# A projection block's stores issued by ScalarE behind its evictions, in a hybrid attention and mLSTM layer

## The reference, cut to what matters

```python
xn = rms_norm(h, norm_mix_w[l])
proj = jnp.einsum('bsd,de->bse', xn, w_in[l])
(da_q, da_k, da_v, ml_q, ml_k, ml_v, ml_i, ml_f, ml_o, gate_pre) = jnp.split(proj, split_idx, axis=-1)
oa = diff_attention(qa, ka, va, lam, cos, sin)     # 8 heads, causal, two softmaxes a head
hm = mlstm_chunkwise(qm, km, vm, i_pre, f_pre)     # 8 heads, after a short causal convolution
merged = g[:, :, 0] * ya + g[:, :, 1] * yb         # ya, yb: both outputs projected
h = h + jnp.einsum('bsd,de->bse', merged, w_out[l])
u = jax.nn.relu(jnp.einsum('bsd,df->bsf', hn, w_ff1[l]))
h = h + jnp.einsum('bsf,fd->bsd', u * u, w_ff2[l])
```

## Time and profile before

| | |
|---|---|
| median of 3 runs | 1978.75 us |
| profiled execution | 1974.37 us, of which the span is 1972.6 us |
| granted TensorE clock, mean | 0.997 |
| TensorE (PE) matmuls | 1910.6 us, 97% |
| VectorE (DVE) | 1190.3 us, 60% |
| ScalarE (ACT) | 965.5 us, 49% |
| GpSimd (POOL) | 383.9 us, 19% |
| stores `proj_d<-ev` | 128 of 256 KB |

### The profile page before, as it was taken

One profiled execution on the slowest core, in us unless ns is written; L12 is line 12 of the kernel. 1 busy time (PEld: TensorE's weight loads), 2 busy tenths in 40 slices (PEclk: granted clock), 3 DMA queues, 4 the chain that ended last, 5 costly groups with the idle time before them and its releaser, 6 DMA issues. The chain is left out here.

```text
span 1972.6 us, 26074 instructions
## 1 busy us (share of the span) xinstructions
PE 1910.6 (97%) x9378; PEld 1598.0 (81%) x9378; DVE 1190.3 (60%) x1538; ACT 965.5 (49%) x1634; POOL 383.9 (19%) x211
## 2 busy tenths in 40 slices
PE   5999999999999999989999999999999999999998
PEld 4788888788888787878888888888888888888886
DVE  6755666566575757553412112278777677789874
ACT  4355565556465556544434322226666765533341
POOL 4221212112121121211213444440000000021002
PEclk9999999999999999999999999999999999999999
DMA  5562747554444546274446453655686686563422
GB/s 152 87 179 57 162 68 152 78 131 107 119 108 115 117 68 166 57 160 99 65 97 213 134 154 92 222 187 211 208 297 225 223 298 211 209 231 132 159 82 86
DMA packets 207826, 291.79 MB, mean 148 GB/s; under 512 B 36841, under 2 KB 127593, under 8 KB 200833
## 3 DMA queue, kind: packets, MB, share of 16 engines
q1 hardware_dynamic: 195856, 282.21, 51.6%
q10 hardware_dynamic: 11888, 8.49, 1.3%
HBM read 203.56 MB, written 87.10 MB: 147 GB/s over the span
## 5 line engine op out<-in xcount | busy, mean ns | idle before, releaser
L730 PE MATMUL gp<-r1h,w_hi 128*128 128x512 f32 x1152 | 454.6, 395 | 6.0 <-ACT ev L1076 3.7
L732 PE MATMUL gp<-r1h,w_lo 128*128 128x512 f32 x1152 | 450.0, 391 | 0.0
L731 PE MATMUL gp<-r1l,w_hi 128*128 128x512 f32 x1152 | 449.4, 390 | 0.0
L1973 POOL TENSOR_TENSOR w_lo<-w_raw,w_hi 128x1024 fp32r<-128x1024 f32 x87 | 218.3, 2510 | 852.2 <-ACT w_hi L1071 852.2
L730 PEld LDWEIGHTS gp<-r1h,w_hi 128*128 128x128 f32 x1152 | 216.8, 188 | 49.7 <-issue 4.1
L732 PEld LDWEIGHTS gp<-r1h,w_lo 128*128 128x128 f32 x1152 | 216.5, 188 | 46.2
L731 PEld LDWEIGHTS gp<-r1l,w_hi 128*128 128x128 f32 x1152 | 216.9, 188 | 41.8
L991 PE MATMUL scores<-xh,qh 128*128 128x512 f32 x512 | 200.1, 391 | 0.6 <-ACT res L1372 0.6
L995 PE MATMUL scores<-xh,ql 128*128 128x512 f32 x512 | 199.2, 389 | 0.0
L993 PE MATMUL scores<-xl,qh 128*128 128x512 f32 x512 | 199.2, 389 | 0.0
L1214 ACT ACTIVATE pr<-scores,nb 128x256 f32<-128x256 f32 (+7 forms) x128 | 93.8, 738 | 118.3 <-DVE nb L1607 116.7
(11 more groups left out here) (342 smaller groups left out, 3745.5 us busy)
## 6 DMA issues: line engine op xcount, KB each, us to landing
xraw<-xo_d SPq DMA_DIRECT2D x54, 1024.0 KB, 5.2
proj_d<-ev SPq DMA_DIRECT2D x128, 256.0 KB, 4.3
rq<-in_w_ff SPq DMA_DIRECT2D x32, 1024.0 KB, 7.8
w_raw<-in_w_in SPq DMA_DIRECT2D x56, 512.0 KB, 9.0
xo_d<-res SPq DMA_DIRECT2D x78, 256.0 KB, 3.3
xo_d<-ring SPq DMA_DIRECT2D x60, 256.0 KB, 2.9
pr<-proj_d SPq DMA_DIRECT2D x16, 512.0 KB, 5.4
gt<-proj_d SPq DMA_DIRECT2D x32, 256.0 KB, 2.8
```

What stands on the lines that cost most here:

```text
L730: pe.matmul(gp[half][:], wh[slot][:, k, :], mh[:, k, t], start=(k == 0), stop=False)
L731: pe.matmul(gp[half][:], wh[slot][:, k, :], ml[:, k, t], start=False, stop=False)
L732: mm = pe.matmul(gp[half][:], wl[slot][:, k, :], mh[:, k, t], start=False, stop=(k == KT - 1))
L1973: pool.tensor_tensor(wl[slot][:], raw[slot][:], wh[slot][:].bitcast(F32), ALU.subtract).then_inc(w_split, 1)
```

## The change

`evac` no longer counts `ev_ready` up: it issues the store itself, on ScalarE's queue. `store` and its calls on SP are gone. In the gate part, where a pair of `oa` loads stood behind each half's store, SP waits on `gp_free` for the same eviction instead. The wait on `st` ahead of the eviction stays, and so do the waits on `st` ahead of SP's loads of `proj_d`.

```diff
-        ev_ready = [sem(f"ev_ready{i}") for i in range(2)]
...
-            def store(n, behind=None):
-
-                for i in range(2):
-                    sp.wait_ge(ev_ready[i], n + 1)
-                    sp.dma_start(proj_d[bass.ds(n, 1), :, i * HALF:(i + 1) * HALF].rearrange("a p n -> (a p) n"),
-                                 ev[i][:]).then_inc(st[i], 16)
-                    if behind:
-                        behind(i)
...
             def head_round(h, att, first=False, second=False, last=False):
                 for b in range(HB):
-                    if b >= 2 or not first:
-                        store(h * HB + b - 2)
...
             for j in range(16):
-                store(N_GATE + j - 2, oa_loads if j == 14 else None)
+                if j == 14:
+                    for i in range(2):
+                        sp.wait_ge(gp_free, 2 * (N_GATE + j - 2) + i + 1)
+                        oa_loads(i)
...
-            for k in range(2):
-                store(N_PA - 2 + k)
...
                 act.activation(ev[half][:], gp[half][:], ACT.Copy).then_inc(gp_free, 1)
                 act.wait_ge(gp_free, 2 * n + half + 1)
-                act.sem_inc(ev_ready[half], 1)
+                act.dma_start(proj_d[bass.ds(n, 1), :, half * HALF:(half + 1) * HALF].rearrange("a p n -> (a p) n"),
+                              ev[half][:]).then_inc(st[half], 16)
```

## The result

| | before | after |
|---|---|---|
| median, 12 runs each, same chip | 1978.10 us (1974.50 to 1983.69) | 1985.43 us (1981.85 to 1989.06) |
| profiled execution, and its span | 1974.37 us, 1972.6 us | 1984.96 us, 1983.1 us |

The ratio is 1.0036, 95% interval [1.0027, 1.0045]: 7.1 us slower by the ratio, 7.3 us by the medians, where 3.7 us were forecast. The time is inside the likeliest case's own range.

What follows compares the result with a forecast made beforehand. TensorE bounds the kernel, its matmuls covering 780.55 of 808 us, so only its waits through ScalarE count. Added 13.0 less removed 9.3 is 3.7 us, on the 1978.75 us median 1982.5 us; range 1970 to 1993.

Steps and rivals of the forecast that it cites:

- the likeliest case: Added 13.0 us and removed 9.3 us nearly balance: 1982.5 us, own range 1976 to 1988, chance 0.42.
- The price of an issue: On ScalarE's list, one store issue costs between 0.34 and 0.51 us, taken as 0.43 us.
- k2: Issue behind eviction k2 delays the exponential and TensorE's L885, already late: all of 0.43 us a round arrives.
- k3: Issue behind eviction k3 delays `w_hi`, so `w_lo`, `nb` and L885, which has no slack: 0.43 us a round.
- k4 and k5: Issues make ScalarE 0.69 us late, passed through `otmp` and tile 5's exponential to `atl`; less 0.12 slack, 0.57 us a round.
- k7: Issue behind eviction k7 delays `ath` and the splitting behind it; TensorE already stalls on that `atl`: 0.43 us a round.
- Together 3.96 + 3.64 + 1.7 = 9.3 us: Gain: waits ahead of k2 in three rounds, the gate part's stall at 877.79 us, and its lower clock vanish.
- The third rival: Stores land as late on ScalarE's queue: none of the 9.3 us goes, 13.0 come, 1991.8 us; chance 0.08.
- What is late next there: nothing on SP: Where store waits vanish, no SP item behind the removed store is late next, so the 9.3 us count as gained.
- The wait that SP gets in the gate part is ... nothing: SP's new gate-part wait is for the eviction whose store it waited for before, so it costs nothing.
- SP's long issues hold ScalarE's: Slower rival: ScalarE's issue near k2 waits for SP's long row-load issue, 8.4 us more, 1990.9 us; chance 0.25.
- The transfers gain more: Faster rival: round 3's `qraw` load lands in time, another 4.6 us gained; 1970 to 1975, say 1971 us; chance 0.25.

Runs made afterwards that it cites:

- run 1: The kernel before, but ScalarE issues the stores of k2, k3, k5 and k7 in the seven rounds, SP all others: 1985.13 us, ratio 1.0037.
- run 3: The kernel before, stores on SP, plus a 4 KB DMA to a scratch tensor issued by ScalarE behind each eviction of the rounds: 1995.19 us, ratio 1.0085.
- run 7: The changed kernel, with the waits and store issues of k2, k3, k4, k5 and k7 moved behind work TensorE waits for: 1968.65 us, ratio 0.9955 to before.
- run 9: The kernel before, with ScalarE's wait for its own eviction and signal to SP moved later for k2, k3, k4, k5 and k7: 1972.64 us, ratio 0.9961.
- run 5: The kernel before, but ScalarE issues the stores of k0, k1, k10 and k11 of each round and the first gate block: 1974.98 us, ratio 0.9985.
- run 4: The kernel before, but ScalarE issues the stores of k0 and k1 of each round and the first gate block: 1979.81 us, ratio 1.0011.
- run 8: The changed kernel, but SP issues the 32 stores of the gate part, ScalarE those of the eight heads: 1984.35 us, ratio 1.0036 to before.

## Why the prediction was right, and where it was not

- **The price of an issue** (0.43 us in place): right. 0.25 to 0.68 and 0.33 to 0.76 us. Runs 1, 3, 7 and 9 show that it is the place that costs: with five of each round's twelve issues set later, a round is as short as without any issue in these places (103.75 and 103.66 us).
- **k2** (0.43): 0.36 in the changed kernel, 0.38 alone. Right.
- **k3** (0.43): 0.30. Mechanism as said, somewhat smaller.
- **k4 and k5** (0.57, on `atl`): ScalarE was 0.69 us late there, as worked out, but the way was another. The step "it passes this on, through the exponential of tile 5 to `atl`" overlooked the `w_hi` behind k5. `w_lo` and the `kqs` operation behind it on GpSimd are late with it, VectorE's `nb` lasts until that ends, and TensorE stalls ahead of it, on `scores` for `pr`. The slack of 0.12 us at `atl` doesn't count on that way: 0.70 us. GpSimd and VectorE after, in round 5; `nb` ends at 599.46 us, and the first exponential starts at 599.50:

```profile
594.69 2.40 POOL L1963 TENSOR_TENSOR w_lo<-w_raw,w_hi 128x1024 fp32r<-128x1024 f32 x1 [20.09 <-ACT w_hi L1060]
597.05 2.39 POOL L1998 TENSOR_TENSOR kqs<-kqs,sg 128x1024 f32<-128x1024 f32 x1
```

```profile
597.75 1.71 DVE L1597 TENSOR_SCALAR nb<-mx 128x2 f32<-128x2 f32 x1
```

- **k7** (0.43): 0.41. Right.
- **Not predicted**: 0.18 us on `vs`. In run 5, where ScalarE issues k10 and k11 as well, the longest wait there is 0.7 us too, in run 4 0.5: it came with them. So the round's 1.94 us are 1.77 from the four places and 0.18 from elsewhere: that the total fits 1.86 so well is in part luck.
- **"Together 3.96 + 3.64 + 1.7 = 9.3 us" go.** The 3.96 us ahead of k2 went, but the reason given, that the store leaves SP's list, holds only for the 0.64 us of round 3. In rounds 6 and 7 (3.32 us) SP had issued k0's store 0.2 us behind the eviction's end, and run 4, which took it off SP, kept the waits. They go if the store is issued right behind the eviction and the eviction comes 2.07 us earlier, which k10's and k11's issues brought about by accident. So that these 3.32 us went is luck. The third rival, "the store lands as late on its own queue", had 0.08; its mechanism was true (12.6 us and 12.6 us), its result not.
- **"What is late next there: nothing on SP"** for the stall at 878 us: this step failed. I had looked only at SP. GpSimd's `w_lo` was late there as well: it ended at 876.99 us, only 1.5 us before TensorE went on at 878.53. With the store out of the way it became the next wait, 2.53 us, and the lower clock stayed. How much of the 2.53 us comes from ScalarE's later `w_hi` was not measured. Of 5.3 us expected, the gate part gave 0.90.
- **"The wait that SP gets in the gate part is ... nothing"**: failed by 1.34 us. The loads that stood between stores are issued in one run of 10.71 us of issues, and ScalarE waited 7.61 us for one of them, before 6.29. Run 8, with these stores on SP, has 6.04 us there and 45.44 us in that stretch.
- **The rivals.** SP's long issues hold ScalarE's: false, 399 ns was the longest of them all. The Trainium skill's rule of an exclusive lock ("Perfetto Trace Analysis", "DMA Instruction — HWDGE (DVE, Sync)") didn't show between these two queues, in the twelve pairs above. The transfers gain more: in part. `qraw` still waited 2.64 us in round 3 (before 3.96), and the granted clock over that round was 1.00 instead of 0.98, so 1.7 us were not lost. But the places' cost came on top, TensorE waited 1.5 instead of 0.6 us for the load `pr<-proj_d`, and the round took as long as before.

Summed: round 1 and the rounds 8.25 us (13.0 - 3.96 = 9.0 expected), the gate part +0.44 (-5.3 expected), the rest of the program +1.9 in the one execution profiled. That is 10.6 us from profile to profile. The rounds were right within 0.8 us; the gate part was not, and with it put right the sum would have been 5.7 us larger: 9.4 us. The medians, 7.3 us apart, show part of that. The rest is a matter of the clock. Of the 23 executions of the kernel before that stand beside run 1, the nine with a mean granted clock of 0.997 took 1975.1 us in the mean, the six with 0.995 took 1980.3. The profiled one is of the first kind (0.997, 1974.37 us), but the median, 1978.1 us, is not. The changed kernel's twelve all had 0.996 to 0.998. So its ordinary executions lose less to the clock than those of the kernel before; why was not tested. The prediction had a gain of this kind only in its faster rival. It brought the time nearer to the forecast, which for the likeliest case is luck.

Open: why the load of `qraw` comes late in round 3 of every kernel, by 2.3 to 5.1 us (the round takes 107 to 111 us, in part by a lower clock behind it in some), why k0's store in rounds 6 and 7 takes 12 to 14 us to land and 7 to 10 in round 5, why the same stall on `w_lo` is followed by a lower clock in one kernel and not in another, and why the clock falls near 1948 us.

## What to carry to other kernels

An issue costs what the place in its engine's list makes of it: here 0.3 to 0.7 us on the path of the engine that bounds the kernel in four places of a round, nothing a few operations further on. Before a wait is counted as gained, ask of every engine, not only the one it was on, what arrives next; and before a transfer is said to land sooner, take issue and landing apart, because another queue moves only the first. The same holds of a wait for one's own result with a signal behind it: look for those in front of critical work.

## What was not expected of the hardware

- A store's way from the start of its issue to landing was as long on ScalarE's queue as on SP's, which carries nearly all other transfers: 12.6 us and 12.6 us for k0's store of round 6.
- Moving an engine's operation by 0.44 us moved another engine's result by 2.07 us, since GpSimd's long operation holds the VectorE operation that starts behind it (1.22 us become 3.30 or 3.41).
- Waiting for the end of an eviction and one signal behind it cost ScalarE 0.33 us ahead of `w_hi`, which in run 9 starts without idle time; with five of these a round set behind other work, a round was 0.8 to 0.9 us shorter.
